# A hybrid attention, RWKV and convolution backbone on one core: the RWKV part as one interleaved program, residuals in halves, norms on columns, a parallel first stage

## The reference, cut to what matters

```
def reference(x, c, ctx, c_ctx, mod_w, mod_b, norm_g, mlp_w1, mlp_w2, ab_w_in, ab_w_out, ...):
    for i in range(2):
        sh_a, sc_a, gt_a, sh_m, sc_m, gt_m = split(silu(c) @ mod_w[i] + mod_b[i], 6)     # "modulation", 6 x 1024
        hl = rms_norm(xl, norm_g[i, 0]) * (1 + sc_a) + sh_a                              # the context likewise in layer 0
        if i == 0: yl = window attention (8 heads) and RWKV-7 (8 heads, both directions), one projection in, one out
        else:      yl = (gate_b * conv3(gate_c * u)) @ w_out, with gate_b, gate_c, u = split(hl @ w_in, 3)
        xl = xl + gt_a * rms_norm(yl, norm_g[i, 1])
        hm = rms_norm(xl, norm_g[i, 2]) * (1 + sc_m) + sh_m
        xl = xl + gt_m * rms_norm(square(relu(hm @ mlp_w1[i])) @ mlp_w2[i], norm_g[i, 3])
    return xl
# RWKV, per head and direction, 64 x 64 state S:
#   S = S * w_t + (S a_t) b_t^T + v_t k_t^T,   y_t = S r_t;   first over the context, then over the latent tokens
```

## Time and profile before

| what | us |
|---|---|
| median of 3 runs | 2277.02 (2267.87 to 2283.71) |
| the profiled execution, its own time | 2284.38 |
| span of its trace, first to last instruction | 2282.6 |
| PE busy, with 15,546 matmul instructions | 2020.2 (89%) |
| POOL busy | 928.1 (41%) |
| DVE busy | 882.4 (39%) |
| ACT busy | 581.5 (25%) |
| matmuls of `keep_warm` (L175), busy | 350.5 |
| clock of PE granted, mean over the span | 0.892 of full |

### The profile page before, as it was taken

How to read it: one execution, slowest core, us unless ns; L and a number is a source line. 1 busy time by engine, 2 the same in 40 slices (tenths; PEclk the granted TensorE clock), 3 DMA queues, 4 the chain that set the end, 5 groups by cost and what they waited for, 6 DMA issues and landing times. The chain is left out here.

```text
span 2282.6 us, 37183 instructions
## 1 busy us (share of the span) xinstructions
PE 2020.2 (89%) x15546; PEld 1501.3 (66%) x15546; DVE 882.4 (39%) x1372; ACT 581.5 (25%) x830; POOL 928.1 (41%) x625
## 2 busy tenths in 40 slices
PE   7799799689688878969888899999989888999996
PEld 2588477465366646637656488888758665888884
DVE  0312467544444264445335622122440756121125
ACT  2323344320221032022022323233132214232230
POOL 0523011293158039217615444444354444444442
PEclk9899899795697589569768899999999999999998
DMA  6311000032013003102302122222212121222221
GB/s 236 122 56 55 19 1 0 1 118 70 1 59 129 1 4 131 55 1 76 112 5 74 37 92 105 98 92 92 74 56 97 68 74 56 101 103 92 92 99 48
DMA packets 23310, 159.96 MB, mean 70 GB/s; under 512 B 2576, under 2 KB 3216, under 8 KB 4624
## 3 DMA queue, kind: packets, MB, share of 16 engines
q1 hardware_dynamic: 21600, 151.86, 18.9%
q10 hardware_dynamic: 1584, 6.19, 0.7%
HBM read 155.94 MB, written 2.10 MB: 69 GB/s over the span
## 5 line engine op out<-in xcount | busy, mean ns | idle before, releaser
L207 POOL TENSOR_TENSOR v<-raw,v 128x512 fp32r<-128x512 f32 x320 | 416.3, 1335 | 512.2 <-ACT v L195 429.2
L224 PE MATMUL bank<-hm,v 128*128 128x512 f32 x2304 | 535.4, 393 | 20.2 <-DVE hm L1623 11.0
L224 PEld LDWEIGHTS bank<-hm,v 128*128 128x128 f32 x2304 | 434.8, 190 | 121.4 <-issue 16.6
L175 PE MATMUL bank<-cst 128*128 128x512 f32 (+2 forms) x680 | 350.5, 636 | 36.2 <-ACT Pn L857 24.0
L224 PE MATMUL bank<-hid,v 128*128 128x512 f32 x1536 | 349.5, 389 | 0.0
L224 PEld LDWEIGHTS bank<-hid,v 128*128 128x128 f32 x1536 | 288.3, 188 | 59.9
L195 ACT ACTIVATE v<-raw 128x2048 fp32r<-128x2048 f32 x73 | 139.9, 1916 | 418.7 <-PE bank L224 418.7
L175 PEld LDWEIGHTS bank<-cst 128*128 128x128 f32 x680 | 142.6, 240 | 141.9 <-issue 95.8
L1251 POOL TENSOR_TENSOR raw<-raw,cs 128x2048 f32<-128x2048 f32 x40 | 144.4, 3610 | 140.7 <-PE bank L1036 140.7
L224 PE MATMUL bank<-h,w 128*128 128x512 f32 x888 | 166.1, 350 | 13.7 <-POOL w L207 12.7
L224 PEld LDWEIGHTS bank<-h,w 128*128 128x128 f32 x888 | 141.9, 190 | 38.4 <-issue 14.9
(11 more groups left out here) (274 smaller groups left out, 2564.9 us busy)
## 6 DMA issues: line engine op xcount, KB each, us to landing
raw<-w_in SPq DMA_DIRECT2D x143, 1024.0 KB, 4.8
xres<-x_in ACTq DMA_DIRECT2D x1, 2048.0 KB, 9.2
out_T<-xres ACTq DMA_DIRECT2D x8, 256.0 KB, 2.0
kkT<-ctx_in ACTq DMA_DIRECT2D x1, 1024.0 KB, 13.7
csa<-csa_in SPq DMA_DIRECT2D x1, 960.0 KB, 4.6
cst<-cst_in ACTq DMA_DIRECT2D x1, 928.0 KB, 17.0
lw<-lw_in SPq DMA_DIRECT2D x4, 128.0 KB, 4.6
g<-g_in SPq DMA_DIRECT2D x1, 256.0 KB, 2.6
```

The source lines that it names most:

```text
L175: nc.tensor.matmul(out[:, 0:width], K("ones"), cst[:, 0:width], start=True, stop=True)
L207: i = nc.gpsimd.tensor_tensor(W[1][n % 2][:, k:k + 2], raw[n % 2][:, k:k + 2], W[0][n % 2][:, k:k + 2].bitcast(F32), SUB)
L224: last = nc.tensor.matmul(bank(b(s, m), 0, hi - lo), W[w][s][:, k, m * P:(m + 1) * P], H[h][:, k, lo:hi], start=(k == 0 and w == h == 0), ...
```

## The change

The change rewrites a good half of the program. Its parts:

1. `pool_lo` makes the residual in two instructions, half a block each, instead of four.
2. First stage: the 8 modulation blocks get 8 places in SBUF (raw buffers and tensors that are not in use yet), so that 7 loads are issued at once. The operand is padded to 32 columns (`pairs`), and products of 4 channel tiles go to 4 column groups of PE. The norm is made on columns (`token_sums`, `over_partitions`). The first projection block takes its channel tiles one by one for both output tiles, and its residual is made ahead.
3. Projection: the columns are reordered so that the first four blocks are for latent tokens alone (before two), then six for all tokens.
4. RWKV: loop, blocks and barriers are gone; one straight program for four pairs, in which the state steps of pair p-1 and the features of pair p+1 stand between the instructions of the inverse of pair p. The state step is one product and one DVE instruction per direction (before: two products in sequence and three DVE instructions). `keep_warm` is not used. 24 modulation blocks instead of 40 pass here, 6 per pair. Part of the tensors lie in x, which is loaded again at the end.
5. The other 16 modulation blocks (second layer) pass through POOL in the first MLP (`late_product`, `late_sum`), one per two weight blocks, and PE sums them in the `norms` after it (`late_columns`).
6. `norms`: sums over channels by `token_sums` (x as the weights, one column of ones moving) into 4 columns, square root and reciprocal on 128x4, then `over_partitions` (4 matmuls) back to 128x512 in PSUM; the additions to x all on DVE and no longer in part on POOL; fewer `keep_warm`.
7. Convolution: the first output block follows in the same stage, from tensors of its own (`hc`), with DVE making the residual of each tile behind its convolution.

```diff
-        for k in range(0, KT, 2):
-            i = nc.gpsimd.tensor_tensor(W[1][n % 2][:, k:k + 2], raw[n % 2][:, k:k + 2],
-                                        W[0][n % 2][:, k:k + 2].bitcast(F32), SUB)
+        for k in range(0, KT, 4):
+            i = nc.gpsimd.tensor_tensor(W[1][n % 2][:, k:k + 4], raw[n % 2][:, k:k + 4],
+                                        W[0][n % 2][:, k:k + 4].bitcast(F32), SUB)
...
+    def token_sums(pe, src, out, start, stop, groups=TG):
+        for g in range(groups):
+            last = nc.tensor.matmul(out[:, g:g + 1], src[:, g * P:(g + 1) * P], K("ones", 0, 1), start=start, stop=stop)
+        return last
+    def over_partitions(pe, cols, out, groups=TG):
+        for g in range(groups):
+            last = nc.tensor.matmul(out[:, g * P:(g + 1) * P], cols[:, g:g + 1].to_broadcast([P, P]), K("ident"),
+                                    start=True, stop=True)
...
+                for n in range(EARLY - 1):
+                    sp.dma_start(early[n], A["wm0"][n]).then_inc(early_in[n], 16)
...
-                pe_block(pe, S_IN + 1, W, hT, parts=both[:1])
-                with pe.Fori(0, (NB - 3) // 2) as turn:
+                for j in range(1, 4):
+                    pe_block(pe, S_IN + j, W, hT, parts=both[:1])
+                with pe.Fori(0, (NB - 5) // 2) as turn:
...
+            def key_products(p):
+                pool.wait_ge(sig_ready, NP * p + NP)
+                pool.wait_ge(kp_ready, p + 1)
...
+            for p in range(PAIRS):
+                key_products(p)
+                pool.wait_ge(at_ready, p + 1)
+                if p:
+                    pool.wait_ge(mod_done, p)
+                for t in range(TURNS):
+                    modulation(S_MOD + TURNS * p + t, t)
...
+            def state_step(p, s):
+                if s > 1:
+                    pe.wait_ge(z_ready, 2 * STEPS * p + 2 * (s - 1))
+                for d in range(2):
+                    for h in range(2):
+                        ...
+                        last = nc.tensor.matmul(bank(6, at, at + Q)[r], Am[r, d, s * Q:(s + 1) * Q], z, start=True,
+                                                stop=True)
...
+                for lv in range(LVL):
+                    first_product(p, lv, 0)
+                    step(2 * lv + 1)
+                    transposes(p, lv, 0)
+                    if lv < 2:
+                        piece(4 * lv)
+                    if lv == 3:
+                        bonus(p)
+                    first_product(p, lv, 1)
+                    ...
+                    transposes(p, lv, 1)
+                    ...
+                    second_product(p, lv, 0)
+                    step(2 * lv + 2)
+                    ...
+                    second_product(p, lv, 1)
...
+            for p in range(PAIRS):
+                chunk_matrices(p)
+                inverse(p)
+                results(p)
+            pe.wait_ge(g_ready, 2 * PAIRS)
+            for s in range(1, STEPS + 1):
+                state_step(PAIRS - 1, s)
+            state_output(PAIRS - 1)
...
+                        pool_lo(pool, n0 + 2, W, up)
+                        if late is not None:
+                            late_product(turn)
+                        pool_lo(pool, n0 + 3, W, up)
+                        if late is not None:
+                            late_sum(turn)
...
-                    link(nc.vector.reciprocal(rst[0][:], rst[0][:]))
+                    nc.vector.reciprocal(rcol[:, 0, :], rcol[:, 0, :]).then_inc(inv_ready, 1)
...
+        dense(S_CIN, 12, lambda t: gates[:, t, :] if t < 2 * KT else None, W, h,
+              beside=convolution, following=projection, behind=rounded)
```

More of the change, by code:

```diff
@@ L341, in _ @@
[L341 to L352 removed]
+                        g = 32 * (k % 4)
@@ new lines, in modulation, with fold @@
+                        last = nc.tensor.matmul(bank(4 + n // 2, at, at + 256)[g:g + 32], pairs[:, k, :],
+                                                early[n][:, 256 * k:256 * (k + 1)], start=k < 4, stop=k >= 4)
+                    last.then_inc(early_used, 1)
+                def fold(j):
+                    pe.wait_ge(rows_ready, j + 1)
+                    for t in range(4 * j, 4 * j + 4):
+                        last = nc.tensor.matmul(cols[:, 2 * t:2 * t + 2], rows[j][:, (t % 4) * P:(t % 4 + 1) * P],
+                                                K("fold"), start=True, stop=True)
+                    last.then_inc(folded, 1)
@@ new lines, in _ @@
+                fold(1)
+                modulation(6)
+                fold(2)
+                modulation(7)
+                fold(3)
+                keep_warm(2, bank(0))
+                pe.wait_ge(split_ready[S_IN % 2], nth(S_IN))
+                for k in range(KT):
+                    pe.wait_ge(h_ready[k % 2], k // 2 + 1)
+                    for m in range(2):
+                        for w, e in ((0, 0), (0, 1), (1, 0)):
+                            last = nc.tensor.matmul(bank(2 * m), W[w][S_IN % 2][:, k, m * P:(m + 1) * P],
+                                                    hT[e][:, k, C:N], start=k == w == e == 0,
+                                                    stop=(k == KT - 1 and w == 1))
+                        if k == KT - 1:
+                            last.then_inc(tile_done[S_IN % 2][m], 1)
@@ L1740, in build @@
     out_proj.close()
+    drw.close()
     mix.close()
```

1424 lines of the change are left out of this document (785 added, 639 removed).

## The result

| | before | changed |
|---|---|---|
| median of four runs, us | 2280.36 (2267.87 to 2285.31) | 1816.07 (1812.71 to 1830.51) |
| ratio | | 0.798, 95% interval 0.793 to 0.804 |
| profiled span, us | 2282.6 | 1815.1 |

What follows compares the result with a forecast made beforehand. PE bounds the MLPs, projection and convolution's product; waits bound RWKV. The terms -386 - 26 - 12 - 12 - 4 - 11 = -451 from 2284.4 gave 1833, kept as 1834 us; 8 in 10 range 1760 to 1940.

Steps and rivals of the forecast that it cites:

- Inverse: RWKV, inverse of a pair, with steps, feature matmuls and bonus in it: 40 us, against 43.2 before.
- I take 26: RWKV, results of a pair: small matmuls at 20 to 50 ns give 17 to 39 us, taken as 26.
- the 398 us: RWKV stretch: first features 27, four pairs of 90, minus 9 for first and last pair, end 20; 783.8 before.
- rival 2: RWKV: interleaving works better than priced, unseen patterns at 20 ns, 75 us per pair, 1774 us in all; chance 0.25.
- will be late next: RWKV: the last results, or DVE's dependent chain of mask, product and addition in the inverse, would be late next; no size.
- Projection 140: Sign in the changed profile: projection stretch at 140 us; its term was -12 us, from 96 matmuls fewer.
- stand in PE's idle places: Second double norm: the late modulation's 32 column sums, twice 0.11 to 0.21 us each, fill PE's idle time.
- up to twice that beside POOL: Convolution's seam: DVE's chain, 3.55 us per tile plus 0.7, at most doubles beside POOL; 14 us instead of 25, -11.
- The halves: Residuals in two instructions instead of four: 0, as POOL's saving is hidden; +3 us at most from holding DVE longer.
- The clock (1): Rival: the clock stays at half in RWKV without `keep_warm`, 120 us per pair, 1954 us in all; chance 0.12.
- POOL's hold on DVE (3): Rival: RWKV's DVE operations each wait for a POOL multiplication, 130 us more per pair, 2354 us in all; chance 0.02.
- The steps did not hold up the inverse (4): Rival 4 claimed steps wait in PE's queue and hold up the inverse: 118 us per pair, 1946 in all; chance 0.06.

Runs made afterwards that it cites:

- POOL light: The changed kernel with the modulation's multiplication and two of its three additions on POOL left out in the RWKV stage; 1836.3 us.

## Why the prediction was right

**The total is nearer than its largest term.** RWKV gave 40 us more than forecast, and the other stretches together 23 us less; that these cancel in part, to 18 us, is luck. The interleaving itself works as told.

**RWKV, by its parts.** Chunk matrices: 22 forecast, 20.3, 22.4, 22.1 and 19.3 measured. Inverse: 40 forecast, 39.3, 40.2, 39.3 and 35.2 measured. Results: 26 plus 2 for seams forecast, 17.9, 18.4, 19.8 and 19.9 measured. So the step that was mis-sized is "I take 26": of the matmuls whose pattern no row showed, priced between 20 and 50 ns, 480 start 15 to 17 ns apart and 160 (state output, E and F) 28 ns apart; the masked values in the chunk matrices (50 ns assumed) start 18 ns apart. The results are 9 us per pair, 36 of the 44 us by which the 398 us written for the changed stretch were too many. The rest is mainly the features alone (21.7 for 27), chunk matrices and inverse (10 together) and the end (18.3 for 20), with the "- 9" for the first and last pair taken back. The pair's 78.6 us on average lies just below the band of the forecast (80 to 105) and above the 75 of rival 2: the mechanism is the forecast's, with rival 2's price for the small matmuls.

**The inverse came out right from terms that miss both ways.** The 40 us were summed as PE's work alone. The terms as written give 38: a level of 5.1 us with two steps of 1.0 together is 6.1, and the sum took 6.5. In the second pair PE spent 17.0 us on the products (20.3 written), 8.0 on the transposes (6.5), 3.5 on the steps (5), 6.7 on the features (5.2), 0.95 on the bonus and 4.0 waiting, for which nothing had been put down: 40.2. PE's work is most of it, as forecast; the chain on DVE, which "will be late next", ended none of these waits there, and up to 5.7 us of them in other inverses.

**What hiding gave.** Steps in the inverse instead of behind it: 38 us. Features: 47. The filler of the old steps: 78 by itself. These 163 us don't explain the 426. Four times the parts of the earlier trace rows against the parts above give an estimate of where the rest lies: the steps are 210 us less (228 to 18), the features 115 (137 to 22), E, F, G with the output and the barriers 74 (150 to 76), chunk matrices and inverse 31. Of the 210, filler and hiding are 116, which leaves some 94 for the new algebra of the step (one product and one operation on DVE in place of two and three) and for ten steps in place of twelve: a step alone takes 1.27 us, where the old one took 4.75 with filler and 2.6 without. No run took that algebra alone, so its share is argued, not shown; nor did one take the barriers and the other filler alone.

**Small terms.** First stage (-24.8 for -26; its written steps end at 62 and not 64 us, measured 66.0), projection (-10.6 for -12; the sign "Projection 140" should have read 146, measured 147.9), first and third double norm (-3.4 and -3.9 for -4), last norm (-2.7 for -4) and the first MLP (0 with PE at 1.00, POOL 81% busy) hold. The **second double norm** failed at the sentence that the 32 column sums "stand in PE's idle places": at the lower clock PE had no idle place there, two instructions of 0.21 us per sum lie on the path, 8 us. The **seam** failed at 14 us: its DVE chain was priced at "up to twice that beside POOL", but single operations took four times theirs (2.8 for 0.69). The halves, priced at 0 and "+3 at most", cost 3.1 us in the seam against quarters (6.3 against eighths), and 8 us in the kernel before.

**Rivals.** The clock (1) did not fall: 0.96 to 1.00 in the pairs without any `keep_warm`; in RWKV it fell for longer only where a chain stands alone, in the features, the last steps and the two kernels that put them apart. POOL's hold on DVE (3) struck now and then (4.3 us once), not at every mask. The steps did not hold up the inverse (4): 40.2 and 39.3 us with them, 39.3 in the first pair, which has none.

## What to carry to other kernels

Put the short serial chain between the instructions of a longer piece of work: ten steps cost 12 us and more alone and 0 to 4 inside the inverse, and PE's clock stayed up there without filler. Before that, delete filler inside a serial loop and look whether the clock there changed at all. Where DVE works on SBUF beside POOL on a path, cut POOL's instructions short; where nothing waits, leave them long, since POOL itself takes longer in short ones. When whole times don't tell two kernels apart, compare the stretches that repeat within a few tenths of a us.

## What the hardware showed

- Independent 64x64 matmuls start 15 ns apart (96 in 1.45 us). The page "TensorE: Matmul & The Clock Gate" (section "Wait — 56ns, not 53.3ns?") has 25 ns as the least distance; the measurement decides.
- PE can be busy and its clock stay down: in the second double norm PE ran, mostly one-column, matmuls nearly without a gap from 1186.6 to 1219.2 us, and the granted clock was at its lower level from 1185.6 to 1226.6 (an expectation above says 1196 to 1237), 6 us into the wide matmuls that follow. In the kernel with the late sums moved, with four wide `keep_warm`s in their place, 24 us ahead of the moved sums were left at the lower level.
- The same code took 1816 and 1830 us on two chips. In the first stage the eight small matmuls of one fold took 1.05 us in the changed kernel's profile and 1.87 in POOL light's:

```profile
42.80 1.05 PE L368 MATMUL bank<-cst,kk 128*128 128x2 f32 x8 [0.72 <-ACT kk L314]
```

```profile
44.13 1.87 PE L368 MATMUL bank<-cst,kk 128*128 128x2 f32 x8
```

 The clock column reads 1.00 in both stretches, so this rests on the durations; 16 matmuls of 128x256 beside them also took 1.07 and 1.93 us. So a few us seem to come from when the clock rises, and no edit of a few us can be judged by the whole time here.
